# The S5 stage of a hybrid encoder: strips on two 64-row tiles, Toeplitz rows from the diagonal on, states written with j innermost

## The reference

```python
# u = rmsnorm(x); 64 groups of 16 features; 64 complex states a group
lam_bar = exp(lam * step)
b_bar   = ((lam_bar - 1.0) / lam)[..., None] * b
bu      = einsum('blgn,gpn->blgp', u, b_bar)
states  = associative_scan(s_t = lam_bar * s_{t-1} + bu_t)         # over the 512 tokens
y = einsum('gnp,blgp->blgn', c, states).real + d * u
y = gelu(y)
y = y * sigmoid(y @ glu_w + glu_b)
x = x + y
```

## Time and profile before

| | |
|---|---|
| Time, median of 3 runs | 1279.61 us (1279.23 to 1279.71) |
| The profiled execution | 1278.21 us, of which its span is 1276.4 |
| TensorE busy | 1240.6 us, 97% of the span |
| VectorE, ScalarE, GpSimd busy | 671.7, 462.0, 64.8 us |
| S5 stage, up to the GLU's first matmul | 101.9 us |
| DMA moved | 121.03 MB, mean 95 GB/s |

### The profile page before, as it was taken

The page is one execution under the profiler, slowest core; times in us unless marked ns, Lnnn a source line. Parts: engine busy times, 40 slices in busy tenths (PEclk is TensorE's granted clock), DMA queues, the critical chain, the costliest instruction groups (busy, mean ns, idle before and its releaser), DMA issues.

```text
span 1276.4 us, 16013 instructions
## 1 busy us (share of the span) xinstructions
PE 1240.6 (97%) x6277; PEld 1034.5 (81%) x6277; DVE 671.7 (53%) x785; ACT 462.0 (36%) x486; POOL 64.8 (5%) x82
## 2 busy tenths in 40 slices
PE   3889999999999999999999999999999999999998
PEld 3778888888888888888888888888888888888886
DVE  8997754344444444646655465634454444444443
ACT  5635433333333333333333333422333333332232
POOL 6940000000000000000000000000000000000000
PEclk9999999999999999999999999999999999999999
DMA  5373333332312334323232133233232323323331
GB/s 115 100 144 123 99 99 99 99 99 90 105 58 90 105 90 138 107 66 107 66 99 83 57 107 96 69 96 93 74 119 80 102 94 99 99 68 90 93 110 66
DMA packets 141039, 121.03 MB, mean 95 GB/s; under 512 B 5720, under 2 KB 132880, under 8 KB 141008
## 3 DMA queue, kind: packets, MB, share of 16 engines
q1 hardware_dynamic: 138832, 116.40, 29.5%
q10 hardware_dynamic: 2176, 4.20, 1.7%
HBM read 114.29 MB, written 2.10 MB: 91 GB/s over the span
## 4 chain that ended last, share of the span: by engine, by line
PE 94%; ACTq 2%; ACT 2%; DMA 1%; DVE 1%; issue 0%; SPq 0%; DVEq 0%
PE bank L709 27%; PE bank L711 27%; PE bank L710 27%; PE bank L809 2%; PE bank L808 2%; PE bank L807 2%; ACTq L434 2%; DMA s<-in_x_dram 1%; PE bank L835 1%; PE bank L837 1%; PE bank L836 1%; PE bank L846 1%; PE bank L820 0%; PE bank L821 0%; ACT s_states L900 0%; PE bank L537 0%
## 5 line engine op out<-in xcount | busy, mean ns | idle before, releaser
L709 PE MATMUL bank<-u_hi,w_hi 128*128 128x512 f32 x960 | 374.9, 391 | 0.0
L711 PE MATMUL bank<-u_hi,w_lo 128*128 128x512 f32 x960 | 373.6, 389 | 0.0
L710 PE MATMUL bank<-u_lo,w_hi 128*128 128x512 f32 x960 | 373.5, 389 | 0.0
L1186 DVE TENSOR_TENSOR w_lo<-w_raw,w_hi 128x2048 fp32r<-128x2048 f32 x112 | 256.4, 2290 | 165.7 <-ACT w_hi L900 165.6
L900 ACT ACTIVATE w_hi<-w_raw 128x2048 fp32r<-128x2048 f32 x112 | 214.0, 1910 | 319.1 <-PE bank L711 314.0
L709 PEld LDWEIGHTS bank<-u_hi,w_hi 128*128 128x128 f32 x960 | 180.2, 188 | 37.8 <-issue 0.7
L710 PEld LDWEIGHTS bank<-u_lo,w_hi 128*128 128x128 f32 x960 | 180.2, 188 | 37.6 <-issue 0.5
L711 PEld LDWEIGHTS bank<-u_hi,w_lo 128*128 128x128 f32 x960 | 180.2, 188 | 37.5
L709 PE MATMUL bank<-h_hi,w_hi 128*128 128x512 f32 x352 | 136.9, 389 | 0.0
L710 PE MATMUL bank<-h_lo,w_hi 128*128 128x512 f32 x352 | 136.9, 389 | 0.0
L711 PE MATMUL bank<-h_hi,w_lo 128*128 128x512 f32 x352 | 136.9, 389 | 0.0
(11 more groups left out here) (220 smaller groups left out, 1321.6 us busy)
## 6 DMA issues: line engine op xcount, KB each, us to landing
w_raw<-in_ret_w_qkvg_dram SPq DMA_DIRECT2D x24, 1024.0 KB, 4.9
w_raw<-in_ffn_w_gate_dram SPq DMA_DIRECT2D x22, 1024.0 KB, 5.2
w_raw<-in_ffn_w_up_dram SPq DMA_DIRECT2D x22, 1024.0 KB, 5.1
w_raw<-in_ffn_w_down_dram SPq DMA_DIRECT2D x32, 704.0 KB, 4.1
w_raw<-in_ret_w_o_dram SPq DMA_DIRECT2D x8, 1024.0 KB, 5.1
w_raw<-in_s_glu_w_dram SPq DMA_DIRECT2D x4, 1024.0 KB, 5.5
s<-in_x_dram ACTq DMA_DIRECT2D x8, 256.0 KB, 8.5
s_w<-in_x_dram SPq DMA_DIRECT2D x1, 2048.0 KB, 7.6
```

The source lines that it names most:

```text
L709: pe.matmul(o, w_hi[w][:, w_cols], hi, start=first, stop=False)
L710: pe.matmul(o, w_hi[w][:, w_cols], lo, start=False, stop=False)
L711: return pe.matmul(o, w_lo[w][:, w_cols], hi, start=False, stop=end)
L1186: dve.tensor_tensor(w_lo[s][:, :], w_raw[:, s, :], w_hi[s][:, :].bitcast(F32), ALU.subtract).then_inc(w_lo_ready[s], 1)
```

## The change

It changes only how the strips, the Toeplitz matrix and the states are made and moved; the output is the same function.

- `fb` loses its zeros: [128, 2, 32, 16] in place of [.., 32], and VectorE writes the B tables straight into it. ScalarE's four copies into it, and the wait for them, go.
- `strips(k)` uses two tiles of 64 rows, one per half: 16 matmuls of 64 rows with 16 output rows each (PSUM rows 0 and 64) in place of 8 of 128 rows, and 8 in place of 4 for D. `strip_out(k)` makes two copies of 16 rows x 512 in place of one of 32 rows.
- `toeplitz(queue, part, steps)` moves both halves of a row block in one transfer, and only from the diagonal on: 32 transfers of 16 rows, 2 x (8 - r) x 512 bytes a row. Part 0 and 1 are issued by SyncE's queue alone, of parts 2 and 3 the even r by SyncE and the odd r by ScalarE. The zeros below the diagonal are written by seven transfers that SyncE issues ahead of the load of x.
- `s5_input_out` copies in the order chunk, re/im, j: four neighbouring floats are written at a time, and PSUM is read with 128 floats between them.
- The strips lie in `w_raw`'s second half only, so the first GLU unit can be loaded after part 0 is issued. ScalarE and VectorE split it earlier.
- TensorE's order is strips(4); y_inputs(0), (1); strips(5); y_inputs(2), (3); strips(6); y_inputs(4), (5); strips(7); y_states(0, 0); y_states(1, 1); y_transposed(0 to 3); the rest as before.
- GpSimd clears `d_diag`, `d_gain` and the zeros in place of `fb` and the pads; SyncE waits for that ahead of four small loads.

```diff
-        def toeplitz_half(queue, part, half):
+        def toeplitz(queue, part, steps):
             for k in (2 * part, 2 * part + 1):
                 b, fill = S5_AT[("strip", k)]
                 queue.wait_ge(bank_free[b], fill + 1)
-            row = 2 * N * (part // 2) + N * half
-            for r in range(STEPS):
-                first = STEPS - 1 - r
-                queue.dma_start(toep[N * r:N * r + N, half, part, :, :, :].rearrange("p t j n -> p (t j n)"),
-                                strip[row:row + N, part % 2, first:first + STEPS, :, :].rearrange("p t j n -> p (t j n)")
+            rows16 = slice(2 * N * part, 2 * N * part + N)
+            for r in steps:
+                queue.dma_start(toep[N * r:N * r + N, :, part, r:, :, :].rearrange("p h t j n -> p h (t j n)"),
+                                strip[rows16, :, 0:STEPS - r, :, :].rearrange("p h t j n -> p h (t j n)")
                                 ).then_inc(toep_loaded[part], 16)
...
+            sp.wait_ge(d_zeroed, 2)
...
+            sp.wait_ge(zeros_set, 1)
+            b, fill = S5_AT[("u", 7)]
+            sp.wait_ge(bank_full[b], fill + 1)
+            for r in range(1, STEPS):
+                cols = r * PART * N
+                sp.dma_start(toep[N * r:N * r + N, :, :, 0:r, :, :].rearrange("p h q t j n -> p (h q) (t j n)"),
+                             repeated(zeros[:, 0:cols], 1, 2 * NPART)).then_inc(toep_zeroed, 16)
...
-            for part in range(NPART):
-                toeplitz_half(sp, part, 0)
-            for s in range(2):
-                for part in (s, 2 + s):
-                    sp.wait_ge(toep_loaded[part], 16 * 2 * STEPS)
-                load_unit(s, 0, glu_v[:, :, 256 * s:256 * s + 256], KT, 256)
+            toeplitz(sp, 0, range(STEPS))
+            sp.wait_ge(toep_zeroed, 16 * (STEPS - 1))
+            load_unit(0, 0, glu_v[:, :, 0:256], KT, 256)
+            toeplitz(sp, 1, range(STEPS))
+            toeplitz(sp, 2, range(0, STEPS, 2))
+            toeplitz(sp, 3, range(0, STEPS, 2))
+            for part in range(NPART):
+                sp.wait_ge(toep_loaded[part], 16 * STEPS)
+            load_unit(1, 0, glu_v[:, :, 256:512], KT, 256)
...
                 for i in range(JB):
                     for ri in range(2):
-                        pe.matmul(o[:, P * i:P * i + P], fb[:, ri, JB * k + i, :],
-                                  r_tc[:, ri, JB * k + i, :, :], start=(i == 0 and ri == 0), stop=False)
+                        for half in range(2):
+                            rows64 = slice(64 * half, 64 * half + 64)
+                            pe.matmul(o[half][:, P * i:P * i + P], fb[rows64, ri, JB * k + i, :],
+                                      r_tc[rows64, ri, JB * k + i, :, :], start=(i == 0 and ri == 0), stop=False)
...
-                copy(states[:, 1:CH + 1, :, JB * SLOT[k]:JB * SLOT[k] + JB].rearrange("p c r j -> p j r c"),
-                     ps[:, :].rearrange("p (j r c) -> p j r c", j=JB, r=2)).then_inc(free, 1)
+                copy(states[:, 1:CH + 1, :, JB * SLOT[k]:JB * SLOT[k] + JB],
+                     ps[:, :].rearrange("p (j r c) -> p c r j", j=JB, r=2)).then_inc(free, 1)
...
-                copy(strip[rows32, k % 4 // 2, STEPS - 1:, JB * (k % 2):JB * (k % 2) + JB, :],
-                     ps[rows32, :].rearrange("p (j t n) -> p t j n", j=JB, t=STEPS)).then_inc(free, 1)
+                for half in range(2):
+                    last = copy(strip[2 * N * (k // 2):2 * N * (k // 2) + N, half, :, js, :],
+                                ps[64 * half:64 * half + N, :].rearrange("p (j t n) -> p t j n", j=JB, t=STEPS))
+                last.then_inc(free, 1)
...
             strip_out(4)
             strip_out(5)
-            toeplitz_half(act, 2, 1)
+            toeplitz(act, 2, range(1, STEPS, 2))
             strip_out(6)
             act.activation(small[:, 25:26], eps[:, :], ACT.Gelu_apprx_tanh)
+            split_weights(0, 0)
             strip_out(7)
-            toeplitz_half(act, 3, 1)
+            toeplitz(act, 3, range(1, STEPS, 2))
```

More of the change, by code:

```diff
@@ L354, in trunk @@
         tc_ready = sem("tc_ready")
-        pads_zeroed = sem("pads_zeroed")
+        zeros_set = sem("zeros_set")
+        toep_zeroed = sem("toep_zeroed")
         diag_ready = sem("diag_ready")
@@ L605, in strips @@
                 ps, full = s5_open("strip", k)
-                o = ps[2 * N * (k // 4):2 * N * (k // 4) + 2 * N, :]
+                o = [ps[64 * half:64 * half + N, :] for half in range(2)]
                 for i in range(JB):
                     for ri in range(2):
-                        pe.matmul(o[:, P * i:P * i + P], fb[:, ri, JB * k + i, :],
-                                  r_tc[:, ri, JB * k + i, :, :], start=(i == 0 and ri == 0), stop=False)
+                        for half in range(2):
+                            rows64 = slice(64 * half, 64 * half + 64)
+                            pe.matmul(o[half][:, P * i:P * i + P], fb[rows64, ri, JB * k + i, :],
+                                      r_tc[rows64, ri, JB * k + i, :, :], start=(i == 0 and ri == 0), stop=False)
                 for i in range(JB):
-                    mm = pe.matmul(o[:, P * i:P * i + N], ident[0:2 * N, 0:2 * N], d_diag[:, JB * k + i, :],
-                                   start=False, stop=(i == JB - 1))
+                    for half in range(2):
+                        rows16 = slice(64 * half, 64 * half + N)
+                        mm = pe.matmul(o[half][:, P * i:P * i + N], ident[rows16, 64 * half:64 * half + N],
+                                       d_diag[rows16, JB * k + i, :], start=False, stop=(i == JB - 1))
                 mm.then_inc(full, 1)
@@ L680, in y_inputs @@
                     pe.matmul(o, u[:, jj, half, :], toep[:, half, jj // PART, :, jj % PART, :], start=(jj % 4 == 0), stop=False)
-            pe.wait_ge(toep_loaded[0], 16 * 2 * STEPS)
+            pe.wait_ge(toep_zeroed, 16 * (STEPS - 1))
+            pe.wait_ge(toep_loaded[0], 16 * STEPS)
             y_inputs(0)
             y_inputs(1)
-            strips(6)
+            strips(5)
             pe.wait_ge(seg_done, 1)
-            pe.wait_ge(toep_loaded[1], 16 * 2 * STEPS)
+            pe.wait_ge(toep_loaded[1], 16 * STEPS)
             y_inputs(2)
             y_inputs(3)
+            strips(6)
+            pe.wait_ge(toep_loaded[2], 16 * STEPS)
+            y_inputs(4)
+            pe.wait_ge(seg_done, 2)
+            y_inputs(5)
             strips(7)
-            pe.wait_ge(seg_done, 2)
             y_states(0, 0)
-            pe.wait_ge(toep_loaded[2], 16 * 2 * STEPS)
-            y_inputs(4)
-            y_inputs(5)
             y_states(1, 1)
@@ L959, in strip_out @@
                 ps, free = s5_full("strip", k)
-                rows32 = slice(2 * N * (k // 4), 2 * N * (k // 4) + 2 * N)
-                copy(strip[rows32, k % 4 // 2, STEPS - 1:, JB * (k % 2):JB * (k % 2) + JB, :],
-                     ps[rows32, :].rearrange("p (j t n) -> p t j n", j=JB, t=STEPS)).then_inc(free, 1)
+                js = slice(JB * (k % 2), JB * (k % 2) + JB)
+                for half in range(2):
+                    last = copy(strip[2 * N * (k // 2):2 * N * (k // 2) + N, half, :, js, :],
+                                ps[64 * half:64 * half + N, :].rearrange("p (j t n) -> p t j n", j=JB, t=STEPS))
+                last.then_inc(free, 1)
             act.wait_ge(rs_ready, 1)
@@ L981, in _ @@
                 s5_table_out(c, 1)
[L982 to L989, removed]
                 if c == 2:
@@ L1680, in mul @@
                 return pool.tensor_tensor(o, a, b, ALU.mult)
-            pool.memset(fb[:, :, :, :], 0.0).then_inc(fb_zeroed, 1)
-            for s in range(2):
-                zeroed = pool.memset(strip[:, s, 0:STEPS - 1, :, :], 0.0)
-            zeroed.then_inc(pads_zeroed, 1)
+            pool.memset(d_diag[:, :, :], 0.0).then_inc(d_zeroed, 1)
+            pool.memset(d_gain, 0.0).then_inc(d_zeroed, 1)
+            pool.memset(zeros, 0.0).then_inc(zeros_set, 1)
             pool.wait_ge(ident_loaded, 16)
-            step(pool.tensor_tensor(d_mask, ident[0:2 * N, 0:N], ident[0:2 * N, N:2 * N], ALU.add))
+            step(pool.tensor_tensor(d_mask, ident[0:64 + N, 0:N], ident[0:64 + N, 64:64 + N], ALU.add))
             pool.tensor_tensor(pair.rearrange("p (h c) -> p h c", h=2), repeated(ident[:, 0:64], 1, 2),
```

33 lines of the change are left out of this document (13 added, 20 removed).

## The result

The kernel after takes 1284.7 us (1283.8 to 1286.5, 7 runs) where the kernel before took 1279.6: a ratio of 1.0039, 95% interval 1.0028 to 1.0049. I had forecast 1277.5 with a range to 1281.0; the change made the kernel 5 us slower.

What follows compares the result with a forecast made beforehand. The program after 100 us slides as a block, so only an earlier first GLU matmul pays: 1.05 us from S plus 1.1 from the gelus, 2.1 off 1279.6, gives 1277.5 us; range 1276.5 to 1281.0.

Steps and rivals of the forecast that it cites:

- S: Start of the recurrence on VectorE, at 54.30 us before; forecast at 53.25, 1.05 us earlier, with a floor of 52.51.
- The copy into `states` at 0.6: ScalarE's copies into `states` before the recurrence: 0.6 us each in the new order in place of 1.09.
- 1.97 + 0.5: One strip on TensorE: 16 matmuls as 8 overlapping pairs in 1.97 us, plus eight D matmuls in 0.5.
- Zeros, part 0, the first 1 MB unit and part 1 have their issues done by 67 and are hidden: Transfers issued ahead of part 2: all issued by 67 us, costing no time.
- I take 160, so 3.7 us: Part 2's 590 KB at 160 GB/s: 3.7 us plus 1.7 fixed, landing at 78.8 us.
- 79.3 as the sign of being wrong: Upper bound for part 2's landing, in us; a later landing would show the prediction wrong.
- the rival at 0.10: Toeplitz transfers from 16 partitions limited to 98 GB/s: part 2 lands at 81.1, total 1280.9 us; chance 0.10.
- Four issues of about 0.65: ScalarE's four transfer issues between strip_out(7) and the gelus: about 0.65 us each, from 84.5 to 87.1.
- gelus no longer behind eight issues: Between quarter 2 of the recurrence and the transposes: 1.1 us gained, net of the new queue.
- the forecast 99.75: Time in us for the GLU on TensorE: transposes from 89.0 plus 10.73, against 101.86 before.
- My 10.73: Time in us from the first transpose to the GLU on TensorE, taken as unchanged.
- TensorE drops to half clock: Clock falls to 1.2 GHz after the 2.2 us wait for part 2; GLU at 102.8, total 1280.5 us; chance 0.13.

Runs made afterwards that it cites:

- runs 3 to 6: Kernel after with one transfer per half (64), half 1's strip on half 0's rows, 64 partitions away, 64 again, 32 away: 1293.76, 1290.99, 1292.38, 1292.46 us.
- half_same_rows: Kernel after with one transfer per half again (64, 32 issued by each queue), both halves' strips on the same 16 partitions: 1293.76 us, ratio 1.0107.
- no_zeros: Kernel after without its seven zero transfers and the waits for them, blocks below the diagonal not zeroed: 1282.54 us, ratio 1.0017.
- order_only: Kernel after with strips(7) and y_states(0, 0) ahead of y_inputs(4), (5), and ScalarE splitting the first unit behind the four gelus: 1277.92 us, ratio 0.9991.
- sp_only: Kernel after with all 32 Toeplitz transfers issued by SyncE's queue, none by ScalarE: 1283.41 us, ratio 1.0032.

## Why the prediction was wrong

**S.** The copy into `states` at 0.6 was right (598 ns), and so were the strips: 1.92 + 0.37 for one strip against 1.97 + 0.5, the two tiles overlapping. Of the two rules of the Trainium skill on this copy (Advanced Engine Details and Errata, Memory Cachelines) the one for SBUF agrees with the run, 1087 to 598 ns, and the one for PSUM does not. The rule against two row tiles on one bank (TensorEngine Tiling (Array Packing), Gotcha 1: PSUM Pressure) didn't hold here either: the halves wrote different rows of one bank, and their 16 matmuls took 1.92 us, as long as the 8 of the kernel before. With the zeros out of the way S was 52.34, better than the 53.25 of the sum. **The step that failed is "Zeros, part 0, the first 1 MB unit and part 1 have their issues done by 67 and are hidden".** I asked whether the 1.83 MB were in time for y_inputs(0), and not what else would be under way while they moved. They held the DMA engines 0.8 to 0.9 busy from 36 us and 0.95 or more from 40 to 52, stopped TensorE for 2.07 us, and the clock fell behind the stop: S = 56.36, 3.1 us late. Part 1 wasn't hidden either: its last issue ended at 73.1 and not by 67, and y_inputs(2) waited 2.41 us for it. That wait cost nothing here, since TensorE waited for part 2 next.

**The rate.** "I take 160, so 3.7 us" failed too, as the runs 3 to 6 show. Part 2 landed 7.8 us after strip_out(5) (75.44 to 83.3, where I had named 79.3 as the sign of being wrong) and not 5.4; the rival at 0.10 had this rate, 98 GB/s, and I set it aside because it came with a share of 0.56 and so seemed to leave room. In the kernel after the same 98 goes with 0.92. My rate was taken from rows in which the two queues read 32 neighbouring rows. The rival was right that the source partitions set the rate, though not that their number does. It put the time at 1280.9, as it had no late start in it and no slow issues.

**The queues.** "Four issues of about 0.65" took 5.27 us, the eight of ScalarE at a median of 1465 ns each, where the earlier trace rows had 612. Each now moves two halves. I read it as a queue that backs up behind slow transfers: the first of four takes 0.6 to 0.7 us, the later ones up to 2.05. With half as much in each transfer, at 91 GB/s, eight issues took 5.98 us (half_same_rows), 0.75 each; large transfers at the fast rate were not run, so the cause is argued. The gain of 1.1 us, "gelus no longer behind eight issues", was therefore none: four slow issues cost nearly what eight had (6.10 us in the earlier trace rows). And the new order put strips(7), strip_out(7), those issues and the gelus behind part 2. I had written this chain down and priced it at the fast rate and at issues of 0.65.

**The sum along that chain,** against my own steps. Part 2 starts 2.0 us late (strip_out(5) at 75.44, not 73.4), takes 2.5 longer, the strips are 0.4 shorter; from the end of strips(7) to the transposes it is 95.73 - 87.39 = 8.3 us, not 5.7, so 2.6 more: 6.7 late at y_transposed(0). Behind it, to the end of the last transposes, 11.9 and not 10.7, as the first transposes ran at a lower clock (3.47 for 1.97). Together 7.85 us, from the forecast 99.75 to 107.60. (My 10.73 and 99.75 run to that end, and the first GLU record comes 0.25 earlier.) The order carries most of it: with strips(7) ahead of the wait for part 2 the same late zeros, slow transfers and slow issues cost nothing that a run can tell from the kernel before.

**The clock.** The rival "TensorE drops to half clock" put the fall behind the wait for part 2; that wait (2.62 us, before 83.34) left the full rate, and the falls came behind the stop at 47.63 and the 4.37 us before 95.73. Where the same wait was longer, 4.42 us in no_zeros, the clock did fall behind it, to 0.50 from 82 to 84.

## What to carry to other kernels

Before transfers are called hidden, ask what else the DMA engines carry then, and from which partitions they read: a transfer between SBUF partitions runs at the rate of the few that it reads, and such traffic can, as it seems, hold up even the instructions. When fewer transfers move the same data from fewer partitions, price both the bytes and the issue time anew. And put work that doesn't need a late transfer ahead of the wait for it: here the order was worth 6.8 us, three times what came back with the zeros' transfers gone.

## What the runs showed of the hardware that I had not expected

- TensorE stopped for 2.07 us (2.22 in order_only, 2.26 in sp_only) with no releaser, in each of the seven profiles in which the zero transfers run up to about 52 us, and in none of the others. In those seven no 16 KB instruction packet starts between 37.4 and 47.0 us; in the other seven one starts at 41.1 to 42.4.
- The rate of transfers between SBUF partitions depends on the distance between the two groups of source partitions: 155 to 159 GB/s at 64, 93 at 32.
- The issue of a transfer on ScalarE took 0.59 to 2.05 us in the kernel after, the longest while its earlier, slow transfers were under way.
- The clock's falls don't order by the idle time ahead of them alone: it held through 2.62 us before 83.34 and fell behind 2.07 before 49.70.
